# Three norm pairs of a transformer stack: the last feature tile squared straight from its bank, one column sum weighted on TensorE, and two early column sums put ahead of the last dense matmuls

## The reference, cut to what matters

```python
y = swiglu(y, ffn1_w_gate[l], ffn1_w_up[l], ffn1_w_down[l])
h = h + FFN_RESIDUAL_WEIGHT * g1 * rmsnorm(y, ffn1_post_g[l])

y = rmsnorm(h, mix_pre_g[l]) * (1.0 + sc2) + sh2
y = token_mix(y, ...)
h = h + g2 * rmsnorm(y, mix_post_g[l])

y = rmsnorm(h, ffn2_pre_g[l]) * (1.0 + sc3) + sh3
```

## Time and profile before

| | us |
|---|---|
| median of 3 runs | 2247.02 (2246.76 to 2247.05) |
| the profiled execution's own time | 2245.89 |
| its span | 2244.0 |
| PE busy | 2215.1 (99%), 12,700 matmul and 12,700 weight-load records |
| DVE busy | 1314.1 (59%) |
| ACT busy | 848.2 (38%) |
| POOL busy | 246.7 (11%) |
| chain that ended last | PE 91%, DVE 7%, ACT 1%, issue 1% |

### The profile page before, as it was taken

The page is one execution under the profiler, slowest core; times in us unless marked ns, Lnnn a source line. Parts: engine busy times, 40 slices in busy tenths (PEclk is TensorE's granted clock), DMA queues, the critical chain, the costliest instruction groups (busy, mean ns, idle before and its releaser), DMA issues.

```text
span 2244.0 us, 30750 instructions
## 1 busy us (share of the span) xinstructions
PE 2215.1 (99%) x12700; PEld 1812.5 (81%) x12700; DVE 1314.1 (59%) x1967; ACT 848.2 (38%) x1318; POOL 246.7 (11%) x193
## 2 busy tenths in 40 slices
PE   8999999999999999999999999999999999999998
PEld 6888888788777888887788988888887779888887
DVE  6755547668367454548633666664387776644443
ACT  4332223545454223223633443323254564423221
POOL 0000003104032000003110100000134411000001
PEclk9999999999999999999999999999999999999999
DMA  7766642222112366532221246664131112532221
GB/s 305 250 214 221 203 134 97 94 86 68 57 66 83 124 203 217 193 120 77 88 96 57 76 163 227 205 213 140 57 109 67 43 58 98 182 102 102 94 94 38
DMA packets 82362, 287.22 MB, mean 128 GB/s; under 512 B 9136, under 2 KB 12080, under 8 KB 81712
## 3 DMA queue, kind: packets, MB, share of 16 engines
q1 hardware_dynamic: 81360, 283.43, 37.1%
q10 hardware_dynamic: 864, 1.84, 0.2%
HBM read 283.13 MB, written 2.10 MB: 127 GB/s over the span
## 4 chain that ended last, share of the span: by engine, by line
PE 91%; DVE 7%; ACT 1%; issue 1%; DMA 0%; POOL 0%; SPq 0%; DVEq 0%; ACTq 0%
PE bank L308 25%; PE bank L310 24%; PE bank L309 24%; DVE wlo L1785 2%; PE bank L451 1%; PE bank L452 1%; PE bank L453 1%; DVE tmps L2005 1%; PE bank L1016 1%; PE bank L477 1%; PE bank L1032 1%; PE bank L364 1%; PE bank L472 1%; PE bank L358 1%; PE bank L780 1%; PE bank L359 1%
## 5 line engine op out<-in xcount | busy, mean ns | idle before, releaser
L308 PE MATMUL bank<-yhi,whi 128*128 128x512 f32 (+1 forms) x1670 | 652.5, 391 | 0.2 <-DVE ylo L2151 0.2
L310 PE MATMUL bank<-yhi,wlo 128*128 128x512 f32 (+1 forms) x1670 | 644.1, 386 | 0.0
L309 PE MATMUL bank<-ylo,whi 128*128 128x512 f32 (+1 forms) x1670 | 644.1, 386 | 0.0
L1785 DVE TENSOR_TENSOR wlo<-raw,whi 128x1024 fp32r<-128x1024 f32 (+2 forms) x373 | 470.0, 1262 | 248.2 <-ACT whi L1130 247.6
L1130 ACT ACTIVATE whi<-raw 128x1024 fp32r<-128x1024 f32 (+2 forms) x373 | 384.1, 1031 | 310.0 <-PE bank L310 247.3
L308 PEld LDWEIGHTS bank<-yhi,whi 128*128 128x128 f32 x1670 | 313.7, 188 | 78.8 <-issue 15.8
L310 PEld LDWEIGHTS bank<-yhi,wlo 128*128 128x128 f32 x1670 | 313.7, 188 | 63.9
L309 PEld LDWEIGHTS bank<-ylo,whi 128*128 128x128 f32 x1670 | 313.9, 188 | 60.5 <-issue 0.2
L308 PE MATMUL bank<-mlp_ahi,whi 128*128 128x512 f32 (+1 forms) x552 | 206.6, 374 | 0.0
L309 PE MATMUL bank<-mlp_alo,whi 128*128 128x512 f32 (+1 forms) x552 | 206.2, 374 | 0.0
L310 PE MATMUL bank<-mlp_ahi,wlo 128*128 128x512 f32 (+1 forms) x552 | 206.2, 374 | 0.0
(11 more groups left out here) (386 smaller groups left out, 2700.2 us busy)
## 6 DMA issues: line engine op xcount, KB each, us to landing
raw<-in_ada SPq DMA_DIRECT2D x152, 512.0 KB, 4.3
raw<-in_ffn_up SPq DMA_DIRECT2D x88, 512.0 KB, 4.3
raw<-in_mlp_up SPq DMA_DIRECT2D x64, 512.0 KB, 3.2
raw<-in_mlp_dn SPq DMA_DIRECT2D x64, 512.0 KB, 3.2
raw<-in_ffn_dn SPq DMA_DIRECT2D x32, 512.0 KB, 3.3
raw<-in_w_dqkv SPq DMA_DIRECT2D x24, 512.0 KB, 3.3
raw<-in_ffn_dn SPq DMA_DIRECT2D x16, 384.0 KB, 3.5
first<-in_ada SPq DMA_DIRECT2D x8, 512.0 KB, 16.9
```

Source lines behind the costliest of these rows:

```text
L308: e.matmul(out, wh, xh, start=first, stop=False)
L309: e.matmul(out, wh, xl, start=False, stop=False)
L310: mm = e.matmul(out, wl, xh, start=False, stop=last)
L1785: e.tensor_tensor(k.wlo[:, home, at:at + width], raw[:, 0:width], k.f(k.whi[:, home, at:at + width]), ALU.subtract).then_inc(*sig.up("wlo" ...
```

## The change

- **Tile 7 stays in its bank.** In the FFNs, `held` makes tile 7 of all three groups into one bank (`y7`), kept out of the ring from group 0 to group 2. ACT's copy and DVE's two adds of that tile go. In the mixer the copy of tile 7 is no longer made ahead of its squares. ACT squares tile 7 from the bank. DVE's product C z h reads the bank too and now waits for that square. ACT copies the bank to `yac` or `mix_out` later, in `prenorm`, after the second root; `post(7)` waits for it.
- **PE weights.** ACT no longer makes (C z)² of tile 7. PE multiplies the plain square by a column of C² instead of ones: `coef[:, 16:17]`, made once per bridge by a new small DVE step in `coefficients`, off `Dve.bridge`.
- **Early columns.** `bridge_early` makes the columns of tiles 0 to 6 of `hz` and `sq` ahead of the last three matmuls of the last dense unit. It waits there for DVE's and POOL's sums of tile 6.
- **Order in `Pe.bridge`**: cz of tiles 0 to 6, then of tile 7 sq, cz, hz; the filler between the columns and the spread of r goes.
- **DVE's small steps** are regrouped: ((cz r + 2 hz) r) + total, then the maximum with 0; five in place of six, of which the one with hz and three behind it wait for hz.
- ACT's table preparation (`ready_root`, L1162) is ahead of the wait for the last unit.

The diff, cut to its core:

```diff
+    def held(self, st, g, x, kts, late):
+        u = self.count(f"{st}_dn{g}")
+        out = k.banks.at("y7", st) if g else self.bank("y7", st, hold=True)
+        w.wait_ge(*sig.on("wlo", u))
+        for kt in range(kts):
+            w.wait_ge(*sig.on(lo, *key, kt))
+            if late and kt == kts - 1:
+                late()
...
+            e.matmul(out, wh, xh[:, kt, :], start=g == 0 and kt == 0, stop=False)
+            e.matmul(out, wh, xl[:, kt, :], start=False, stop=False)
+            mm = e.matmul(out, wl, xh[:, kt, :], start=False, stop=g == 2 and kt == kts - 1)
+        mm.then_inc(*sig.up("lin", u))
+        if g == 2:
+            k.banks.let_go(("y7", st))
...
-    def wide_column(self, out, sq, first, last):
+    def wide_column(self, out, sq, first, last, weights=None):
+        weights = self.k.ones[:, 0:32] if weights is None else weights
...
-    def bridge(self, st):
+    def bridge_early(self, st):
...
-        out, hz, cz = self.bank("S", st), self.bank("hz", st), self.bank("cz", st)
+        out, hz = self.bank("S", st), self.bank("hz", st)
+        w.wait_ge(*sig.on("dsum", st, 6))
+        self.wide_column(hz, k.tm(0), True, False)
         w.wait_ge(*sig.on("sqadd", st, 6))
         self.wide_column(out, k.tm(4), True, False)
-        w.wait_ge(*sig.on("dsum", st, 6))
-        self.wide_column(hz, k.tm(0), True, False)
+
+    def bridge(self, st):
+
+        w, sig, k = self.w, self.sig, self.k
+        out, hz, cz = k.banks.at("S", st), k.banks.at("hz", st), self.bank("cz", st)
         w.wait_ge(*sig.on("czadd", st, 6))
         self.wide_column(cz, k.tm(6), True, False)
         w.wait_ge(*sig.on("sq", st, 7))
         self.wide_column(out, k.tm(5), False, True).then_inc(*sig.up("tot", st))
+        w.wait_ge(*sig.on("coef", st + "zz"))
+        self.wide_column(cz, k.tm(5), False, True, k.coef[:, 16:17].to_broadcast([128, 32])).then_inc(
+            *sig.up("tot", "cz", st))
         w.wait_ge(*sig.on("hz", st, 7))
         self.wide_column(hz, k.tm(1), False, True).then_inc(*sig.up("tot", "hz", st))
-        w.wait_ge(*sig.on("cz", st, 7))
-        self.wide_column(cz, k.tm(7), False, True).then_inc(*sig.up("tot", "cz", st))
-        self.warm(1, 256)
         self.root(st, 0)
...
+            if gated:
+                self.held(st, g, a, counts[g], (lambda: self.bridge_early(st)) if g == 2 else None)
...
+        self.linear("wout", x, order, late=lambda: self.bridge_early("mix"))
...
+        w.wait_ge(*sig.on("hz", old, 7))
+        self.e.activation(out, k.banks.at(*bank), k.ACT.Copy).then_inc(*sig.up("yac", old, 7, bank=bank))
...
+        e.tensor_tensor(t, cz, r, ALU.mult).then_inc(*sig.up("ssum", "step", st, 0, bank=("cz", st)))
...
+        e.scalar_tensor_tensor(t, hz, 2.0, t, ALU.mult, ALU.add).then_inc(*sig.up("ssum", "step", st, 1, bank=("hz", st)))
...
+        e.tensor_tensor(t, t, r, ALU.mult).then_inc(*sig.up("ssum", "step", st, 2))
...
+        e.tensor_tensor(total, total, t, ALU.add).then_inc(*sig.up("ssum", "step", st, 3))
...
+                    w.wait_ge(*sig.on("sq", st, 7))
+                    self.bridge_product(st, n, k.banks.at("y7", st))
```

More of the change, by code:

```diff
@@ L287, in bank, with linear @@
         return tile
-    def linear(self, tag, x, order=range(8), kts=None, hold=False):
+    def linear(self, tag, x, order=range(8), kts=None, hold=False, late=None):
         w, sig, e, k = self.w, self.sig, self.e, self.k
@@ L298, in linear @@
             w.wait_ge(*sig.on(lo, *st, kt))
+            if late and kt == order[-1]:
+                late()
             self.three(out, u, kt, xh[:, kt, :], xl[:, kt, :], kt == order[0], kt == order[-1])
         return u
+    def held(self, st, g, x, kts, late):
+        w, sig, e, k = self.w, self.sig, self.e, self.k
+        xh, xl, lo, key = x
+        u = self.count(f"{st}_dn{g}")
[4 more added lines that the diff above has]
+            if late and kt == kts - 1:
+                late()
+            slot, at = k.home[u]
+            c = slice(at + 128 * kt, at + 128 * kt + 128)
+            wh, wl = k.whi[:, slot, c], k.wlo[:, slot, c]
+            e.matmul(out, wh, xh[:, kt, :], start=g == 0 and kt == 0, stop=False)
[4 more added lines that the diff above has]
+            k.banks.let_go(("y7", st))
     def three(self, out, u, kt, xh, xl, first, last, kind="lin"):
@@ L563, in wide_column @@
                 mm = self.e.matmul(out[p:p + 32, 128 * j:128 * j + 32], sq[:, 128 * j + p:128 * j + p + 32],
-                                   self.k.ones[:, 0:32], start=first and j == 0, stop=last and j == 3)
+                                   weights, start=first and j == 0, stop=last and j == 3)
         return mm
@@ L660, in down @@
             last = not gated and g == len(counts) - 1
-            for n in range(NT - HALVED[st] if last else NT):
+            for n in range(NT - HALVED[st] if last else NT - 1 if gated else NT):
                 self.linear(f"{st}_dn{g}", a, kts=counts[g])
+            if gated:
+                self.held(st, g, a, counts[g], (lambda: self.bridge_early(st)) if g == 2 else None)
             if last:
@@ L901, in mix @@
         self.pair(["wout", "wout"], x, "yhi", order, lambda kt: mlstm_spreads() if kt == 0 else None)
-        for _ in range(6):
+        for _ in range(5):
             self.linear("wout", x, order)
+        self.linear("wout", x, order, late=lambda: self.bridge_early("mix"))
         self.bridge("mix")
@@ L1229, in bridge_square @@
         k, w, sig = self.k, self.w, self.sig
-        if n == 7:
-            self.ready_root()
         if n >= 2:
             w.wait_ge(*sig.on("sqadd", st, n - 1))
+        if n >= 2 and n < 7:
             w.wait_ge(*sig.on("czadd", st, n - 1))
         self.square("sq", (st, n), k.tm(4 if n == 0 else 5)[:, 0:S], z)
+        if n == 7:
+            return
         w.wait_ge(*sig.on("coef", st + "z"))
@@ L1271, in prenorm @@
                           scale=1.0 / D).then_inc(*sig.up("rsq", sums))
+        old, bank, out = {"ffn1h": ("ffn1", ("y7", "ffn1"), k.yac["ffn1"][:, 7, :]),
+                          "mixh": ("mix", ("u", k.last["wout"]), k.mix_out(7)),
+                          "ffn2h": ("ffn2", ("y7", "ffn2"), k.yac["ffn2"][:, 7, :])}[sums]
+        w.wait_ge(*sig.on("hz", old, 7))
+        self.e.activation(out, k.banks.at(*bank), k.ACT.Copy).then_inc(*sig.up("yac", old, 7, bank=bank))
         for n in range(NT):
@@ L1336, in down @@
                 u = self.unit(f"{st}_dn{g}")
-                if gated and g == 0:
+                if gated and g == 0 and n < 7:
                     w.wait_ge(*sig.on("lin", u))
@@ L1343, in down @@
                         self.prep_to(self.u + NW - 2)
+                    if gated and n == 7:
+                        self.ready_root()
+                        w.wait_ge(*sig.on("lin", u))
+                        self.bridge_square(st, n, k.banks.at("y7", st))
+                        continue
                     w.wait_ge(*sig.on("acc", st, g, n))
@@ L2046, in post @@
         def post(n):
+            if n == 7:
+                w.wait_ge(*sig.on("yac", st, 7))
             e.scalar_tensor_tensor(k.tm(n)[:, 0:S], z(n), C[:, n:n + 1], R, ALU.mult, ALU.mult).then_inc(
@@ L2124, in down @@
                     self.gated(st, g, n, u, v_gate)
-                elif g:
+                elif g == 2 and n == 7:
+                    self.prep_to(self.u + NW - 2)
+                    w.wait_ge(*sig.on("sq", st, 7))
+                    self.bridge_product(st, n, k.banks.at("y7", st))
+                elif g and n < 7:
                     if g == 1:
@@ L2131, in down @@
                     yac = k.yac[st][:, n, :]
-                    if g == 2 and n == NT - 1:
-                        self.prep_to(self.u + NW - 2)
                     e.tensor_tensor(yac, yac, k.banks.at("u", u), ALU.add).then_inc(
@@ L2363, in mix @@
                 self.prep_to(self.u + NW - 2)
-            w.wait_ge(*sig.on("yac", "mix", n))
-            self.bridge_product("mix", n, k.mix_out(n))
+            if n < NT - 1:
+                w.wait_ge(*sig.on("yac", "mix", n))
+                self.bridge_product("mix", n, k.mix_out(n))
+            else:
+                w.wait_ge(*sig.on("sq", "mix", 7))
+                self.bridge_product("mix", n, k.banks.at("u", k.last["wout"]))
     def gla(self):
@@ L2762, in build_program @@
         k.sil = sb("sil", [128, 8])
-        k.coef = sb("coef", [128, 16])
+        k.coef = sb("coef", [128, 17])
         k.stat = sb("stat", [128, 17])
```

24 lines of the change are left out of this document (13 added, 11 removed).

## The result

| | before | after |
|---|---|---|
| median of 4 runs | 2247.03 (2246.76 to 2247.18) | 2261.05 (2260.57 to 2262.25) |
| the profiled execution's own time | 2245.89 | 2262.25 |
| its span | 2244.0 | 2260.4 |

The ratio is 1.0066 (95%: 1.0055 to 1.0078). The change makes the kernel **slower by 14 us, 0.66%**. The forecast was no change, 2246.7, with a range up to 2248.4.

A forecast was written before the change was run, and what follows sets the result against it. PE, 91% of the chain, was taken as the bound. Earlier post(0) less 0.89 us per bridge gained 0.31: 2245.89 became 2245.6, plus 1.13 for the median gave 2246.7 us, range 2244.6 to 2248.4.

The forecast's parts named there:

- The new DVE step in `coefficients`: In each bridge's coefficients: one more DVE step of 0.2 us beside dense work, costing nothing.
- the 0.31: All three bridges together: gain of post(0) less 0.89 each, 0.09 after ffn1, 0.00 after the mixer, 0.22 after ffn2.
- The early columns cost PE time: Ahead of each bridge's last three dense matmuls: 64 records delay T0, when the last dense result is readable, by 0.89 us.
- post(0) at **2.70: In a bridge without a pause: post(0) starts 2.70 us after T0, against 3.68 after ffn1 and 3.59 after the mixer.
- I take the middle, 2.8: After ffn2: PE's pause ends 2.8 us after the new T0, between 2.04 and 3.61, putting post(0) at 4.0.
- the early end named: After ffn2: the pause ends 3.72 us after the first column's start, as before, so 2.04 after the new T0.
- rival 1: After ffn2: the pause goes, post(0) at 2.70, gain there 1.52, in all 1.6; time 2245.4 us; chance 0.28.
- A gain of 0.22: Bridge after ffn2: post(0) moves from 5.11 to 4.0 us, less 0.89 for the early columns.
- rival 4: In the bridges: TensorE's clock falls to 1.2 GHz since a filler is gone; time 2252.4 us; chance 0.02.
- ACT's late copy: Behind the second root, ahead of the first `yhi`: ACT's 0.60 us copy of the bank costs nothing.
- The held bank: In the ring of banks: seven remain, each released within a unit or two, so holding one costs nothing.
- rival 5: Before the last dense matmuls: early columns wait for DVE or POOL, 0.5 us each; time 2248.2 us; chance 0.02.

## Why the prediction was wrong

- **The step that failed** is a cost of nothing: "The new DVE step in `coefficients` is one more of 0.2 us beside dense work: nothing." The step was costed as an instruction, and the column into which it writes was not costed at all. `coef[:, 16:17]` widens a tile, and that moves the hidden tiles by 32 bytes: 2,472 matmuls by 6.7 ns, 16.5 us, some 50 times the 0.31 on which the forecast rested. One unused column in the kernel before cost 17.6 us, and the change with C² put elsewhere gave 2244.67. No rival had it either, since all five were looked for in the bridges. What would have found it: the sizes of all tiles in the diff, and the groups by shape, in which the chain's 91% of PE lie.
- "The early columns cost PE time ... Sum **0.89 per bridge**": right, 0.79 + 0.10.
- "So post(0) at **2.70** without a pause": right, 2.64 after ffn1 and after the mixer. The product began at 0.63 as worked out.
- "I take the middle, 2.8" for the end of the pause: too late. It ended 2.09 behind T0, which is 3.78 behind the first early column; the early end named (3.72 behind the first column, so 2.04) was right. post(0) came 1.07 later (1.2 was taken), at 3.16 in place of 4.0. This term was mis-sized by 0.84, and the case lies between the forecast and rival 1, the pause gone. It came 112 records behind the 64 early ones (103 to 111 were said), within the hz column as said, and the place in the stream did stay.
- The 5.11 from which the term was counted is itself one execution of a time that varies. The mean of post(0) after ffn2 is 5.7 in the eight traces with the old bridge and 3.4 in the five with early columns there. A gain of 0.22 in that bridge was below what one trace could tell.
- The sum for the bridges is 1.04 + 0.95 + 1.95 - 3 x 0.89 = 1.27 by the two profiled executions, and 1.7 with the means of the last point, where the forecast had 0.31; the change without its placement measured 1.8. That is within 0.2%, the prediction's own bound for no change, and so its account of the bridges stood; its account of the kernel did not.
- Three of its sums slipped by some tenths, which decides nothing: rival 4 adds up to 2252.7 and not 2252.4, and by its own terms the range is 2244.8 to 2248.1 (the late end of the pause, 4.8 in place of 4.0, is 0.8 and not 0.6).
- "ACT's late copy ... costs nothing", "The held bank ... nothing", the early columns' waits (rival 5): right. The first T0 is later by 4.41, the 0.89 and the 3.5 of the slower matmuls.
- Rival 4, the fall of the clock, was given 0.02 and a wrong trigger. It does occur, but behind a long pause and not for want of a filler: behind 3.00 and 2.73 us without early columns, and behind 2.42, 2.11 and 1.75 in the kernel before with its tiles moved by 32 and 64 bytes, which has the filler. Behind 1.82, 1.74, 1.59 and all shorter ones the bridge kept 2.4 GHz, so the length of the pause alone does not decide.
- The Trainium skill (Runtime: NRT & Kernel Launch, Instruction fetch mechanics) calls a block's crossing "mostly hidden". It agrees with the traces but for one place: of PE's idle time only the pause after ffn2, 0.32 to 3.00 us, is marked "issue" with more than 0.25 us, out of 101 packets in a trace. By that rule the early columns would be pure cost everywhere; after ffn2 they are not.

Three things stay open. That it is the load of the weights which meets the stream is inferred from moving the one, the other and both; no kernel without weight loads was run. And which load meets which stream is not worked out: the halves that 64 bytes hit, and why `alo` moved alone slows `ahi` too. Nor is it shown what sets the start of the instruction packet, 1.0 to 2.7 us behind the first column, and with it the length of the pause.

## What to carry to other kernels

Before costing a change by its instructions, list every tile whose size it touches and what is allocated behind it: a new column of 4 bytes moved the operands of 2,472 matmuls and cost nine times what the change was worth. A loss in parts of the program that the diff doesn't touch is a sign of placement, and the mean ns of the groups by shape shows it in one view; a pad of the same size in the kernel before settles it. Work put ahead of its time on the bounding engine costs its full length, unless it breaks up a stretch in which that engine runs out of something else.

## What the runs showed of the hardware

- In these kernels a matmul of 512 columns that streams and loads from SBUF steps by 227 ns when the stream and the weights start at the same place modulo 256 bytes (difference 0 or 256), and by 233 ns at a difference of 32 or 128. At 64, the steps behind the three forms `ahi` by `whi`, `ahi` by `wlo` and `alo` by `whi` were 231.7, 229.2 and 226.0 ns, against 226.6.
- After ffn2 PE waits for an instruction packet once 170 or 176 column records are done, and for how long is not constant: 0.32 to 3.00 us in the fifteen traces. It goes on 1.1 to 1.5 us behind the end of the packet.
- Behind the pauses of 3.00, 2.73, 2.42, 2.11 and 1.75 us TensorE was granted its lower level (1.2 GHz) for 3.4 us; behind those of 1.82, 1.74 and less it was not.
- A column of 32 small records takes 0.26 us from its first start to its last when it stands alone, and 0.29 when it stands directly behind another. The weighted column (C², one element spread over 32) has 0.29 in the place of the second, and so has a column of ones in the early pair.
